# Layer norms shifted by four chunks' mean, with compact statistics, in a decoder layer on one core

## The chip, the cores and the metric

One core of one Trainium2 chip. Times are device microseconds (us) of one execution; the median of three runs of the kernel before is 938.13 us (937.85 to 939.4).

## What is computed

One decoder layer for 256 prompt rows and 64 sample rows (8 sequences of 8), width 1024, all fp32. Cut to the parts that matter:

```python
def _layernorm(x, g, b):
    mu = jnp.mean(xf, -1, keepdims=True)
    var = jnp.mean(jnp.square(xf - mu), -1, keepdims=True)
    y = (xf - mu) * lax.rsqrt(var + LN_EPS) * g + b

def mod(t, i):
    return t * (1.0 + ada[:, i, 1, None, :]) + ada[:, i, 0, None, :]

def post(t, y, i):
    return _layernorm(DEEPNORM_ALPHA * t + ada[:, i, 2, None, :] * y, ln_g[i], ln_b[i])

x = post(x, 0.5 * _swiglu(mod(x, 0), f1g, f1u, f1d), 0)
m, st = mixer(mod(x, 1))          # q, k, v, glu projection; attention over a paged cache; convolution
x = post(x, m, 1)
x = post(x, 0.5 * _swiglu(mod(x, 2), f2g, f2u, f2d), 2)
```

## The kernel before, in words

**Layout.** Activations are kept transposed: width over 128 partitions and 8 chunks, 320 rows along the free side (`xT`, `yT`, `uT`, one chunk 128x320). Every product runs in three fp32r matmuls (high x high, high x low, low x high), so each weight unit of 2048 columns of bytes (256 output columns, 1 MB) is loaded to `raw`, rounded to `whi` by ScalarE (`hi`, line 656) and its rest put into `wlo` by VectorE (`lo`, line 973). A unit's product is two halves (cc 0 and 1) of 24 matmuls of 320 columns (`product`, lines 1409 to 1411); `products` (lines 1422 to 1424) does several targets chunk by chunk, as the chunks' high (`mh`) and low (`ml`) parts come from a norm.

**Stages**, each in order on TensorE: adaptive parameters (`ada`), FFN 1 up (UP1, 22 units) and down (DN1, 12 units), input projection (WIN, 10 units, with the prompt's attention between), the cache stage (64 chunks of 1 MB of cached keys and values in a ring of 8 slots, loaded through SyncE's queue; four pairs of sequences, `pair_keys` and `pair_values`), output projection (WOUT, 4 units), FFN 2 (UP2, DN2), and the rows out. The order of each engine is written out by hand; semaphores tie them. SyncE's loads stand in one queue and each waits until its slot is free.

**Slots.** `whi` and `wlo` have two slots, `whi2` and `wlo2` are a third. They share memory with the cache stage's buffers: `whi` with `kT`, `wlo` with `kvw` (ring slots 6 and 7), `whi2` and `wlo2` with `araw` (ring slots 4 and 5, and in FFN 1 the landing place of the ada weights). `slot_w` names the slot of a unit, `slot_before` the unit that must be used up before its high half may be written. Output weights 0 and 1 are loaded before the last values, to `araw`, while values 4 and 5 of the last pair go to `kvw`; so the low half of output unit 0, which is written to `kvw`'s memory, waits until these values are used (`v_used`).

**A norm before.** `add_residual` (lines 1025 to 1027) makes `yT` chunk by chunk from the last products and from `xT`, which GpSimd has scaled by alpha (`scale_x`, line 582). GpSimd sums chunks 0 to 6 (`y_sums`, line 577); TensorE multiplies this sum and chunk 7 with a matrix of 1/1024, which gives the mean in every partition (lines 1498, 1500). VectorE subtracts it in four passes of two chunks (line 1081), ScalarE squares (738), VectorE adds the squares by pairs (1085), TensorE sums them over partitions (1504), ScalarE takes the root (740), VectorE the reciprocal over 128x320 (1088). Then per chunk: scaling (1093), modulation for the next stage from folded parameters (`fold_g`, `fold_b`; 1103 to 1105), high part by ScalarE (745), low part by VectorE (1019), and the new `xT` with gain and bias by ScalarE (747). Between, `keep_clock` gives TensorE matmuls of no use (1494). One low half of the next stage stands between the squares' sums and the reciprocal.

**The end of the cache stage.** `pair_values(3)` works on 8 values as they land. Before the last value `conv_half(0, 0, 4)` does 24 matmuls of output unit 0 on the convolution's chunks; the same of unit 1, in two parts around `attn_turn(3)`, follows the last value. Then the attention's chunks for both units together, then units 2 and 3.

## Time and profile before

| | us |
|---|---|
| median of 3 runs | 938.13 |
| the profiled execution | 937.36 |
| its span | 935.5 |
| TensorE busy | 854.9 |
| VectorE busy | 470.2 |
| ScalarE busy | 343.2 |
| GpSimd busy | 267.1 |

The span runs from the first to the last instruction; the execution's time is 1.9 us longer. Matmuls are pipelined and their shown ends overlap, so distances are read from start to start. An idle time with the engine and line that ended it stands in brackets behind a row. The times of all rows are those of this one execution.

### The profile page before, as it was taken

Reading aid. Unit: us, or ns where it says so; the run is one execution under the profiler, and the core shown is the slowest. Engines: PE = TensorE matmul, PEld = TensorE weight load, DVE = VectorE, ACT = ScalarE, POOL = GpSimd, SP = SyncE. Lnnn points to the kernel's source line nnn. Section 1 sums busy time; section 2 is a strip of 40 time slices with the busy share of each in tenths; the row PEclk is TensorE's granted clock in tenths of the full one; section 3 lists DMA queues with packets and bytes.
Section 4 is the critical chain, followed back from the end, with each engine's and each line's share of the span. In section 5 each row is a group of like instructions: output and inputs, shape, how many; then the busy total and the mean of one; then the engine's idle time right before and its main releaser. Section 6 shows DMA issues by size and latency. Waiting matters only on the chain.

```text
span 935.5 us, 16896 instructions
## 1 busy us (share of the span) xinstructions
PE 854.9 (91%) x6712; PEld 751.9 (80%) x6712; DVE 470.2 (50%) x751; ACT 343.2 (37%) x465; POOL 267.1 (29%) x319
## 2 busy tenths in 40 slices
PE   5699999998799988999986889869889999999997
PEld 3499989997699968988764556538789999999995
DVE  1543433432233379753686776743773454453436
ACT  2323332331222255454443324363363433432223
POOL 2020000000010013999999999600220000000000
PEclk9599999999799999999999999989999999999999
DMA  9957778777677442433998999996414544634301
GB/s 305 350 191 259 231 231 258 230 232 255 206 234 244 150 142 84 152 126 119 348 319 265 365 350 374 348 347 222 134 54 138 171 135 147 195 125 158 124 1 57
DMA packets 181521, 195.87 MB, mean 209 GB/s; under 512 B 11811, under 2 KB 163609, under 8 KB 181445
## 3 DMA queue, kind: packets, MB, share of 16 engines
q1 hardware_dynamic: 174541, 188.47, 61.9%
q10 hardware_dynamic: 6624, 6.33, 2.1%
q8 instruction: 46, 0.75, 0.3%
q14 instruction: 22, 0.18, 0.1%
q0 software_dynamic: 288, 0.14, 0.1%
HBM read 192.09 MB, written 3.17 MB: 209 GB/s over the span
## 4 chain that ended last, share of the span: by engine, by line
PE 78%; DVE 11%; DMA 5%; ACT 3%; issue 2%; SPq 1%; ACTq 0%; DVEq 0%
PE bank L1409 19%; PE bank L1410 18%; PE bank L1411 18%; PE bank L1625 5%; PE bank L1385 3%; PE bank L1650 3%; PE bank L1720 2%; DVE wlo L973 2%; PE bank L1374 1%; PE bank L1422 1%; DVE kT L1214 1%; PE bank L1423 1%; PE bank L1424 1%; DMA raw<-in_w_ada 1%; DMA xrow<-in_x_sample 1%
## 5 line engine op out<-in xcount | busy, mean ns | idle before, releaser
L973 DVE TENSOR_TENSOR wlo<-raw,whi 128x2048 fp32r<-128x2048 f32 (+1 forms) x80 | 190.8, 2386 | 257.6 <-ACT whi L656 256.3
L1409 PE MATMUL bank<-mh,whi 128*128 128x320 f32 x824 | 261.0, 317 | 4.5 <-DVE wlo L973 4.5
L1411 PE MATMUL bank<-mh,wlo 128*128 128x320 f32 x824 | 255.5, 310 | 0.0
L1410 PE MATMUL bank<-ml,whi 128*128 128x320 f32 x824 | 255.4, 310 | 0.0
L656 ACT CAST whi<-raw 128x2048 fp32r<-128x2048 f32 (+1 forms) x80 | 148.5, 1861 | 258.6 <-PE bank L1411 171.3
L1409 PEld LDWEIGHTS bank<-mh,whi 128*128 128x128 f32 x824 | 155.7, 189 | 15.3 <-issue 10.3
L1410 PEld LDWEIGHTS bank<-ml,whi 128*128 128x128 f32 x824 | 155.9, 189 | 0.0
L1411 PEld LDWEIGHTS bank<-mh,wlo 128*128 128x128 f32 x824 | 155.5, 189 | 0.0
L1409 PE MATMUL bank<-hh,whi 128*128 128x320 f32 x352 | 109.7, 312 | 0.0
L1410 PE MATMUL bank<-hl,whi 128*128 128x320 f32 x352 | 108.6, 309 | 0.0
L1411 PE MATMUL bank<-hh,wlo 128*128 128x320 f32 x352 | 108.6, 308 | 0.0
L622 POOL TENSOR_SCALAR tmp<-cbuf,dwT 128x256 f32<-128x256 f32 x90 | 95.4, 1060 | 0.0
L629 POOL TENSOR_TENSOR yT<-yT,tmp 128x320 f32<-128x320 f32 x90 | 81.2, 903 | 7.5
L1409 PEld LDWEIGHTS bank<-hh,whi 128*128 128x128 f32 x352 | 66.0, 188 | 2.5 <-issue 2.1
L1410 PEld LDWEIGHTS bank<-hl,whi 128*128 128x128 f32 x352 | 66.0, 188 | 0.0
L1411 PEld LDWEIGHTS bank<-hh,wlo 128*128 128x128 f32 x352 | 66.0, 188 | 0.0
L577 POOL TENSOR_TENSOR tmp<-yT 128x320 f32<-128x320 f32 x3 | 2.6, 874 | 219.0 <-DVE yT L1027 219.0
L596 POOL TENSOR_TENSOR fold_g<-adaT,par 128x72 f32<-128x72 f32 x2 | 0.6, 316 | 207.9 <-DVE adaT L993 207.9
L866 ACT COPY kT<-bank 128x1024 f32<-128x1024 f32 x32 | 35.6, 1114 | 55.8 <-PE bank L1625 55.8
L714 ACT ACTIVATE tmp<-bank 128x320 f32<-128x320 f32 x44 | 19.3, 438 | 94.4 <-PE bank L1411 87.4
L1214 DVE COPY kT<-bank 128x1024 f32<-128x1024 f32 x30 | 36.6, 1221 | 28.4 <-PE bank L1625 28.3
L1048 DVE TENSOR_TENSOR tmp<-bank,tmp 128x320 f32<-128x320 f32 x44 | 21.4, 487 | 57.4 <-PE bank L1411 37.0
(237 smaller groups left out, 1151.8 us busy)
## 6 DMA issues: line engine op xcount, KB each, us to landing
araw<-in_w_ada SPq DMA_DIRECT2D x28, 1024.0 KB, 5.1
raw<-in_ffn_wg SPq DMA_DIRECT2D x22, 1024.0 KB, 7.1
raw<-in_ffn_wu SPq DMA_DIRECT2D x22, 1024.0 KB, 7.1
raw<-in_ffn_wd SPq DMA_DIRECT2D x16, 1024.0 KB, 6.5
raw<-in_cache_k SPq DMA_DIRECT2D x64, 256.0 KB, 4.7
raw<-in_cache_v SPq DMA_DIRECT2D x60, 256.0 KB, 5.2
raw<-in_w_in SPq DMA_DIRECT2D x10, 1024.0 KB, 5.2
raw<-in_w_ada SPq DMA_DIRECT2D x8, 1024.0 KB, 12.5
```

The costliest lines, as they stand in the source:

```text
L622: pool.tensor_scalar(to[:, 0:SEQ], cbuf[:, c, k:k + SEQ], w, *more)
L629: pool.tensor_tensor(acc_c, acc_c, to, ALU.add).then_inc(conv_ready if last else pool_step, 1)
L656: act.copy(wh(slot_w(phase, u))[:, 0:size], landed(phase, u)[:, 0:size]).then_inc(w_hi, 1)
L866: act.copy(kT_view(k, 0), bank_keys(0)).then_inc(kt_low, 1)
L973: dve.tensor_tensor(wl(slot_w(phase, u))[:, 0:size], landed(phase, u)[:, 0:size], wh(slot_w(phase, u))[:, 0:size].bitcast(F32), ALU.subtra ...
L1214: dve.tensor_copy(kT_view(k, 1), bank_keys(1)).then_inc(kt_high, 1)
L1385: ins = pe.matmul(bank[g:g + QG, b + a_ % 2, 0:UC], cT[:, kk, :], src[:, UC * kk:UC * kk + UC], start=kk < 4, stop=kk >= 4)
L1409: pe.matmul(bank[:, b, 0:T], wh(slot)[:, c], h_, start=(start and n == 0), stop=False)
L1410: pe.matmul(bank[:, b, 0:T], wh(slot)[:, c], l_, start=False, stop=False)
L1411: ins = pe.matmul(bank[:, b, 0:T], wl(slot)[:, c], h_, start=False, stop=(stop and n == len(parts) - 1))
L1625: ins = pe.transpose(bank[:, 2 * half + x // 2, to:to + P], slot[:, at:at + P], ident)
L1650: ins = pe.matmul(out, qb[:, 2 * j + k // 4, h, :], keys[:, :, :, h, :], start=e == 0, stop=e == 1)
```

## The change

Six things, all in one diff:

- **Shift.** After the first half of down unit 7 (of output unit 2 for norm 1) TensorE multiplies the sum of chunks 0 to 3 with the 1/1024 matrix. VectorE subtracts twice that, the mean of these four chunks, from `yT` chunks 0 to 3 and from `xT` chunks 4 to 7, so that all chunks come out shifted by a value near the mean. The variance is then the mean of the squares less the square of the shifted mean d.
- **Sums inside the last units.** ScalarE squares chunks 0 to 5 and GpSimd adds them up while the last units are multiplied (in norm 1 fewer: squares 4 and 5 come after the stage's last high half).
- **Compact statistics.** Sums over partitions go by `spread`: two matmuls of 64 output rows and 160 columns, so that the 320 rows' statistics lie as 128x160, each twice in scale of 1/16. Square of d, variance, root and reciprocal work on 160 columns; two matmuls put the reciprocal back into two banks for the scaling. d itself is summed in full and subtracted from `yT` by passes of two chunks (`centre`) between the scalings. A root of a single column (`warm`) is put ahead of the last squares.
- **Alpha** is multiplied into the gain and bias columns of norms 0 and 1; GpSimd's scaling of `xT` is left for the first stage only.
- **Projection.** WIN uses the slots in the order 2, 0, 1; its unit 0 no longer waits for a down unit, the last unit shares slot 0 with unit 7 and is converted after it. The low half of WIN unit 1 stands between the residuals of chunks 6 and 7 (UP2 unit 1: between chunks 5 and 6). In the output projection the attention's chunks are done unit by unit; the first two units of UP2 are done as four targets together.
- **Swap.** Values 4 and 5 of the last pair go to `araw`, output weights 0 and 1 to `kvw`; the low halves of these are written over the landed weights, with no wait for values. `conv_half(0)` moves to behind value 5, the first half of `conv_half(1)` to behind value 6. In norm 2 VectorE makes every second output chunk.

```diff
 def kv_slot(kvi):
-    return kvi % KV_RING if kvi < KVN - 8 else (0, 1, 2, 3, 6, 7, 2, 3)[kvi - KVN + 8]
+    return kvi % KV_RING if kvi < KVN - 8 else (0, 1, 2, 3, 4, 5, 2, 3)[kvi - KVN + 8]
 def slot_w(phase, u):
     if phase[0] == WIN[0]:
-        return u % 3
+        return 0 if u == WIN[2] - 1 else (2, 0, 1)[u % 3]
 def slot_before(phase, u):
     if phase[0] == WIN[0]:
-        return phase[0] + u - (2 if u < 2 else 3)
+        if u == 0:
+            return -1
+        return phase[0] + u - (2 if u == WIN[2] - 1 else 3)
     if phase[0] == WOUT[0]:
-        return (WIN[0] + 9, WIN[0] + 7, WIN[0] + 8, WOUT[0])[u]
+        return (WIN[0] + 9, WIN[0] + 8, WIN[0] + 6, WOUT[0])[u]
+NORM_BANKS = ((6, 4, 5, 6, 5), (4, 5, 6, 7, 4), (6, 4, 5, 6, 5))
+HG, NSPREAD = 64, T // 2
...
         # SyncE
-                    sp.wait_ge(w_used, WIN[0] + (9, 9, 10, 8)[kvi - RING])
+                    sp.wait_ge(w_used, WIN[0] + (7, 7, 10, 9)[kvi - RING])
-                        sp.wait_ge(v_used, 16 + 5 + u)
-                        sp.dma_start(araw[:, u, :]...)
+                        sp.wait_ge(v_used, 16 + 7 + u)
+                        sp.dma_start(kvw[:, u, :]...)
...
         # GpSimd
+            def late_sum(n):
+                pool.wait_ge(y_ready, 8 * n + 6)
+                pool.wait_ge(shift_ready, n + 1)
+                pool.tensor_tensor(tmp[:, 3, :], yT[:, 4, :], yT[:, 5, :], ALU.add).then_inc(ysum_step, 1)
+            def square_sum(n, q):
+                pool.wait_ge(sq_ready, 8 * n + q + 1)
+                if q > 1:
+                    pool.wait_ge(sqsum_step, 5 * n + q - 1)
+                pool.tensor_tensor(tmp[:, 2, :], tmp[:, 0, :] if q == 1 else tmp[:, 2, :], tmp[:, q % 2, :], ALU.add).then_inc(sqsum_step, 1)
+            def norm(n):
+                y_sums(n)                      # now chunks 0 to 3
+                for q in range(1, 5):
+                    square_sum(n, q)
+                late_sum(n)
+                square_sum(n, 5)
+            pool.tensor_scalar(par1[:, 72:88], par1[:, 72:88], ALPHA, None, ALU.mult)
+            pool.tensor_scalar(par1[:, 96:112], par1[:, 96:112], ALPHA, None, ALU.mult).then_inc(fold_ready, 1)
-            scale_x(1)
-            scale_x(2)
...
         # ScalarE, in down() of the FFNs
+                    if u == 7:
+                        for q in range(4):
+                            square(n, q)
+                    if u == 9:
+                        square(n, 4)
+                        square(n, 5)
+            def norm(n, first, meanwhile=lambda: None):
+                act.activation(warm[:, :], con[:, C_EPS:C_EPS + 1], ACT.Sqrt)
+                for q in range(first, NCH):
+                    square(n, q)
+                act.wait_ge(rest_ready, n + 1)
+                act.activation(tmp[:, 0, 0:NSPREAD], bank[:, NORM_BANKS[n][2], 0:NSPREAD], ACT.Square).then_inc(dsq_ready, 1)
+                act.wait_ge(vd_ready, n + 1)
+                act.activation(tmp[:, 0, 0:NSPREAD], tmp[:, 0, 0:NSPREAD], ACT.Sqrt, scale=16.0 ** -2, ...).then_inc(std_ready, 1)
+                meanwhile()                    # norm 0: high half of WIN unit 2
...
         # VectorE
+            def shift(n):
+                sums = bank[:, NORM_BANKS[n][0]:NORM_BANKS[n][0] + 1, 0:T].to_broadcast([P, 2, T])
+                dve.wait_ge(shift_ready, n + 1)
+                for q in (0, 1):
+                    y = yT[:, 2 * q:2 * q + 2, :]
+                    dve.scalar_tensor_tensor(y, sums, -2.0, y, ALU.mult, ALU.add).then_inc(yc_ready, 1)
+                for q in (2, 3):
+                    x = xT[:, 2 * q:2 * q + 2, :]
+                    dve.scalar_tensor_tensor(x, sums, -2.0, x, ALU.mult, ALU.add).then_inc(xs_ready, 1)
                 # down(), before the low half of unit u + 2
+                    if u == 7:
+                        shift(sub)
                 # output projection
-                if u < 2:
-                    lo(WOUT, u + 2)
-                elif u == 3:
+            lo(WOUT, 2)                        # ahead of the loop
+                if u == 2:
                     lo(UP2, 0)
+                    shift(1)
+                    if n == 1:
+                        lo(WOUT, 3)
+                    if n == 5:
+                        lo(UP2, 1)
                 # norm()
+                dve.tensor_tensor(small[0], bank[:, NORM_BANKS[n][3], 0:NSPREAD], small[0], ALU.subtract).then_inc(vd_ready, 1)
+                dve.reciprocal(small[1], small[0]).then_inc(nr_ready, 1)
+                dve.wait_ge(mean_ready, n + 1)
+                centre(0)                      # centre(1..3) ahead of the scaling of chunks 2, 4, 6
+                dve.wait_ge(spread_mm, 2 * n + 2)
...
         # TensorE, first FFN 2 products
-                        products([(0, ...), (1, ...), (2, ...)], ...)
-                        product(3, slot_w(phase, 1), 1, m_parts(range(NCH))).then_inc(w_used, 1)
+                        products([(2 * x + cc, ...) for x in range(2) for cc in range(2)], ...)
+            def shift(n):
+                pe.wait_ge(ysum_step, 4 * n + 3)
+                pe.matmul(bank[:, NORM_BANKS[n][0], 0:T], lnones, tmp[:, 3, :], start=True, stop=True).then_inc(shift_ready, 1)
             # norm(n), after the last product
+                pe.wait_ge(y_ready, 8 * n + 7)
+                pe.wait_ge(ysum_step, 4 * n + 4)
+                spread(rest, tmp[:, 3, :], 0)
+                pe.wait_ge(sqsum_step, 5 * n + 5)
+                spread(sq, tmp[:, 2, :], 0)
+                spread(rest, yT[:, 6, :], 1)
+                pe.wait_ge(sq_ready, 8 * n + 7)
+                spread(sq, tmp[:, 0, :], 1)
+                pe.wait_ge(y_ready, 8 * n + 8)
+                spread(rest, yT[:, 7, :], 2).then_inc(rest_ready, 1)
+                pe.wait_ge(sq_ready, 8 * n + 8)
+                spread(sq, tmp[:, 1, :], 2).then_inc(var_ready, 1)
+                ...                            # full mean: three matmuls; the reciprocal back: two
+                keep_clock(2, 5)
-            pair_values(3, {2: group_scales, 6: lambda: conv_half(0, 0, NCC)})
-            conv_half(1, 0, 2)
+            pair_values(3, {2: group_scales, 5: lambda: conv_half(0, 0, NCC), 6: lambda: conv_half(1, 0, 2)})
+            conv_half(1, 2, 3)
             attn_turn(3)
-            conv_half(1, 2, NCC)
-            products(first, ...)
+            conv_half(1, 3, NCC)
+            for u in range(2):
+                products(first[2 * u:2 * u + 2], ...)
             ...
+                    if u == 2 and cc == 0:
+                        shift(1)
```

## Rows read from the trace of the kernel before

**Rows 1.** Page, part 1: busy time, share and instructions of each engine.

```profile
PE 854.9 (91%) x6712; PEld 751.9 (80%) x6712; DVE 470.2 (50%) x751; ACT 343.2 (37%) x465; POOL 267.1 (29%) x319
```

**Rows 2.** Busy by stretch (instructions); last: TensorE's granted clock, DMA share, GB/s.

```profile
602.00:622.00 20.00, 16.96 (x230) 9.71 (x230) 8.00 (x15) 13.07 (x22) 0.00 (x0) 1.00 1.09 346
622.00:632.00 10.00, 3.78 (x40) 1.41 (x44) 6.34 (x6) 5.61 (x8) 0.00 (x0) 0.68 1.10 348
680.00:697.00 17.00, 15.52 (x95) 15.24 (x95) 11.67 (x30) 12.03 (x18) 6.69 (x1) 0.90 0.01 2
```

**Rows 3.** TensorE in order of time: start, length, line, [idle before and releaser]; norm 0, projection.

```profile
336.22 0.78 PE L1498 MATMUL bank<-tmp,con 128*128 128x320 f32 x2 [0.56 <-POOL tmp L577]
...
350.07 0.39 PE L1422 MATMUL bank<-mh,whi 128*128 128x320 f32 x1 [2.30 <-DVE ml L1019]
...
364.09 0.31 PE L1424 MATMUL bank<-mh,wlo 128*128 128x320 f32 x1
367.39 0.41 PE L1409 MATMUL bank<-mh,whi 128*128 128x320 f32 x1 [2.99 <-DVE wlo L973]
...
431.36 0.41 PE L1409 MATMUL bank<-mh,whi 128*128 128x320 f32 x1
...
442.71 0.98 PE L1625 MATMUL bank<-con,raw 128*128 128x128 f32 x7
```

**Rows 4.** VectorE in order of time, from norm 0's mean on.

```profile
337.57 3.01 DVE L1081 TENSOR_TENSOR yT<-yT,bank 128x640 f32<-128x640 f32 x4 [1.00 <-PE bank L1500]
...
342.41 2.28 DVE L973 TENSOR_TENSOR wlo<-raw,whi 128x2048 fp32r<-128x2048 f32 x1
344.61 2.15 DVE L1088 RECIPROCAL tmp<-tmp 128x320 f32<-128x320 f32 x1
...
349.44 0.48 DVE L1019 TENSOR_TENSOR ml<-uT,mh 128x320 fp32r<-128x320 f32 x1
...
358.17 1.10 DVE L1019 TENSOR_TENSOR ml<-uT,mh 128x320 fp32r<-128x320 f32 x2
...
359.41 10.12 DVE L973 TENSOR_TENSOR wlo<-raw,whi 128x2048 fp32r<-128x2048 f32 x2
```

**Rows 5.** ScalarE in order of time, norm 0.

```profile
339.36 1.35 ACT L738 ACTIVATE tmp<-yT 128x640 f32<-128x640 f32 x2
...
341.99 1.28 ACT L740 ACT_TABLE_LOAD   x1
```

**Rows 6.** GpSimd in order of time, behind norm 0.

```profile
359.39 6.68 POOL L582 TENSOR_SCALAR xT<-xT 128x2560 f32<-128x2560 f32 x1 [20.54 <-ACT xT L747]
```

**Rows 7.** TensorE, then VectorE, in order of time, end of the cache stage.

```profile
603.15 2.42 PE L1773 MATMUL bank<-yT,con 128*128 128x320 f32 x8
...
623.98 1.07 PE L1720 MATMUL bank<-kvw,pT 128*32 128x256 f32 x16 [3.24 <-DMA kvw<-in_cache_v]
...
631.23 1.94 PE L1720 MATMUL bank<-raw,pT 128*32 128x256 f32 x16 [2.30 <-DMA raw<-in_cache_v]
...
625.19 2.29 DVE L973 TENSOR_TENSOR wlo<-araw,whi 128x2048 fp32r<-128x2048 f32 x1 [4.11 <-PE bank L1720]
```

**Rows 8.** TensorE in order of time, around norms 1 and 2.

```profile
664.99 0.70 PE L1498 MATMUL bank<-tmp,con 128*128 128x320 f32 x2
...
679.16 0.38 PE L1422 MATMUL bank<-mh,whi 128*128 128x320 f32 x1 [2.00 <-DVE ml L1019]
...
696.49 0.41 PE L1409 MATMUL bank<-mh,whi 128*128 128x320 f32 x1 [1.48 <-DVE wlo L973]
...
914.83 0.70 PE L1498 MATMUL bank<-tmp,con 128*128 128x320 f32 x2
```

**Rows 9.** VectorE and GpSimd in order of time, last unit of the output projection.

```profile
658.94 2.29 DVE L973 TENSOR_TENSOR wlo<-raw,whi 128x2048 fp32r<-128x2048 f32 x1
...
659.10 2.86 POOL L577 TENSOR_TENSOR tmp<-tmp,yT 128x320 f32<-128x320 f32 x1 [0.67 <-DVE yT L1027]
662.62 0.88 POOL L577 TENSOR_TENSOR tmp<-tmp,yT 128x320 f32<-128x320 f32 x1 [0.66 <-DVE yT L1027]
```

**Rows 10.** VectorE in order of time, norm 2: the scaling of all eight chunks.

```profile
925.48 3.31 DVE L1093 TENSOR_TENSOR yT<-yT,tmp 128x320 f32<-128x320 f32 x8
```

169 lines of the change are left out of this document (101 added, 68 removed).

## The prediction

> **What bounds the kernel now.** I read the page first: TensorE is busy for 91% of the span, the next engine for half [rows 1]. So the end is set by TensorE's own work and by the places where it waits, and only those can be shortened. The table of stretches then shows that the cache stage is another thing: from 602 to 622 the DMA queues are full (share 1.09) while TensorE is not, and at the end of that stage (1.10) the granted clock drops to 0.68 [rows 2]. Then TensorE's order of time at the three layer norms: each is a hole. In norm 0 its products end at 335.66 (the wait of 0.56 before 336.22), and the next real product is at 350.07, 14.4 us later; norm 1 runs from 664.99 to 679.16, 14.2 us; norm 2 from 914.83 to the end [rows 3, 8]. What fills the hole is VectorE [rows 4]: four subtractions of the mean (3.01), sums of squares, a low half (2.28), a reciprocal over 320 columns (2.15), then scaling and modulation; the low part of chunk 0 starts at 349.44. Behind norm 0 is a second stall of 2.99: the low halves of the input projection's units 2 and 3 took 10.12 us together where one takes 2.28, beside GpSimd's scaling of x from 359.39 to 366.07 [rows 3, 4, 6]. At the end of the cache stage TensorE waits 3.24 us for values 4 of the last pair and 2.30 for values 6, and the first low half of the output projection waits 4.11 us for TensorE [rows 7].
>
> **Scaling of x gone (alpha is folded into gain and bias).** It removes 6.68 us of GpSimd in two places, which cover nothing else. Without it the low half of unit 2 takes 2.2 us from its start.
>
> **Norm 0.** Price list: a matmul of 320 columns against the ones matrix is two records, 0.70 us with the tail of the last, which the next covers: 0.6 [rows 8]. A "spread" sum is two matmuls of 160 columns to different output halves: 0.3 us if they overlap, 0.58 if not; I take 0.35, since the value products, to four outputs of 32 rows, do overlap: 16 records of 256 columns in 1.07, 0.067 each [rows 7], where a full one of 320 takes 0.1476. A reciprocal of 160 columns is between half of 2.15 and that plus a fixed part: 1.15. A centring pass of two chunks is 3.01/4 = 0.75, the shift pass (the same shape with one PSUM source) the same, 1.0 at worst [rows 4].
> The shift matmul adds 0.6 to the products, so they end at 336.25 (P). The shift passes (3 us of VectorE), squares of chunks 0 to 5 and GpSimd's sums lie under products of units 7 to 11, where VectorE is idle for 5 us and more between low halves; free, or up to 1 us if one holds back a low half. The projection's unit 0 now goes to the third weight slot, free early; the low half of unit 1 moves between the residuals of chunks 6 and 7, so y7 is ready at P+1.35 and no longer at P+0.9, for 2.2 us less later. From there, one after the other: last spread 0.4, its square 0.4, subtraction 0.35, root 0.4 (two squares of 640 take 1.35 [rows 5]), reciprocal 1.15, first centring 0.75, then on VectorE two scalings, the modulation of chunk 0, one centring, a scaling, the modulation of chunk 1 and the low part of chunk 0, 3.9 (from the period of 1.52 per chunk: seven low parts lie between 349.44 and the pair at 358.17, plus 0.85 for the centring [rows 4]). TensorE restarts at P+9.0 = 345.25, after 9.0 where it was 14.4: **5.4 less**, 0.6 of it given back to the shift matmul.
> The first projection is 96 matmuls at (364.09 - 350.07)/95 = 0.1476, 14.17 us [rows 3]. VectorE now spends 1.52 + 0.43 per chunk against 1.77 of TensorE, so two short waits come back: +0.6. It ends at 360.0. The low half of unit 2 is then 357.1 to 359.4 and no one waits: the hole of 3.15 between 364.24 and 367.39 is gone. Sum: 5.4 - 0.6 - 0.6 + 3.15 = **7.35**.
>
> **Does that arrive?** The projection behind it is TensorE's work throughout. The last unit runs from 431.36 to 442.71; unit 8, of equal length, begins at about 420, and only then the last unit's high half may start: its low half is there at about 424.7, 6.7 before it is needed [rows 3]. SyncE's queue now holds cached keys 3 until then (old: 415), but keys 4 and 5 may follow at once instead of waiting for 430; key products start at 442.7. All loads of the cache stage wait for slots freed by this chain, so the full DMA stream moves with it. GpSimd's convolution has ended before 602 (no GpSimd work from there on [rows 2]), TensorE needs it at 603.15 [rows 7], and it starts 7 us earlier too.
>
> **Last values and output weights swap.** Loads keep their order and the queue is what they wait for, so values 4 to 7 land when they did. The low halves of the projection's units 0 and 1 no longer wait for values (4.11 gone); they are written over their own landed weights at about 621 and 628. So 24 matmuls can stand between values 5 and 6, where TensorE idles 2.30 [rows 7]. Half of them run at half clock as before. The products behind the conv part start 2.95 earlier, with 0.5 lost since only 6 matmuls cover the last turn.
>
> **Output projection and norm 1.** Unit by unit, unit 0 ends half a product stage earlier; VectorE takes the low half of unit 2 (now behind the low parts) until 645.9, residuals 0 and 1, the low half of unit 3 until 649.75, residuals 2 and 3 until 651.35, then a low half of the next stage. The shift matmul stands behind the first half of unit 2 (651.55) and needs GpSimd's third sum. In the trace a GpSimd sum of 0.88 that began 0.16 after a low half took 2.86, ending 0.76 after it [rows 9]. Here the same happens: the third sum ends at 654.6, TensorE waits **3.05**, then 0.6 for the matmul. Without the block the wait is 0.95. So the stage ends at 2.95 - 3.65 = 0.7 later than now. Then the hole is 8.7 instead of 14.2: 5.5 less. In the first FFN products, four targets together instead of three and one: 14.17 us, 1.7 of half clock as now (0.90 over 17 us [rows 2]), 0.2; but the last 24 matmuls no longer cover activation, high half and low half of unit 2: those end about 3.9 after the last product, where the wait was 1.48 [rows 8]. 20.0 instead of 17.3: 2.7 lost. Net: -0.7 + 5.5 - 2.7 = **2.1**.
>
> **Norm 2.** Shift matmul: 0.6 lost. Reciprocal done at P+3.85, first centring P+4.6; then 3 centrings, 8 scalings and 4 of the 8 affines on VectorE, 7.4: P+12.0. Now the scalings end at 928.8 = P+13.9 [rows 10], and the copies to rows follow on the same engine in both. **2.1 less**, -0.6.
>
> **A rule weighed.** In the trace one change of ScalarE's function table costs 1.28, at 341.99, under VectorE's work [rows 5]; a dummy root now pulls it ahead. But squares now stand between that root and the real one. The Trainium skill (ScalarE: Activation LUTs, Table sets: the hidden batching unit) says that functions come in sets, that a switch costs about 2.7 us, and names relu, copy, identity and abs as present in every set; square isn't in that list. By it, were square missing beside the root, each norm would pay two more switches. The trace speaks against it: the squares from 339.36 ran before the root's load, with the table that Silu had left.
> A second: by the rows the low half beside GpSimd's scaling ran from 359.41 and both ended at 369.53, so about 5.7 us were lost, not the 6.66 that were left of it. The Trainium skill (SBUF — State Buffer, SBUF: two separate sides) has the port locked for the whole instruction; by that rule the pair would have ended at 370.5, and the gain be the same, as TensorE only waits for the first.
>
> **Rivals.** (A) *GpSimd's sums are not blocked* at the output projection: 2.1 more, 925.1. For: the sum may be issued first. Against: rows 9. 0.12.
> (B) *The clock falls* once more than now, behind norm 0 or in the 3 us wait at the output projection: 1.7 each [rows 2], 929 to 930.6. For: norm 1 shows it. Against: the holes are shorter. 0.12.
> (C) *Square and root are in different tables*: two more loads of 1.28 in each norm, one of them in the chain after the variance, the other partly: about 1.6 per norm, 932. 0.06.
> (D) *The cache stage does not move*, because its stream is full from start to end and something that didn't move starts it: 7.35 lost, 934.6. Against: its loads wait for low halves and units of the projection. 0.08.
> (E) *Slower*: the last unit of the input projection. ScalarE does its high half in the midst of exponentials and table loads, VectorE the low half after; TensorE and, through SyncE's one queue, all cached keys behind key 3 wait for it. Up to 6.7 us late costs nothing, each later one its own length; slower than before by over 0.2% needs 6.7 + 11 + 2 = 20 us late: 941. 0.03.
> (F) The stages are shorter in the profile and the end isn't, 937 to 939: 0.04.
>
> **Numbers.** 7.35 + 2.1 - 0.6 + 2.1 = 10.95. The profiled execution took 937.36 (span 935.5), so 926.4; the median of the runs stands 0.8 above it, so the forecast is 927.2 (chance 0.55, own range 925 to 929.5, from the spread sums, 0.25 each, and the wait at the shift). From A to C: 922.5 to 932.5, leaving out D, E, F and tails. 0.2% is about what a measurement can tell from no change: faster 0.92, same 0.04, slower 0.04.
>
> **What would show it.** Holes of 9.0 and 8.7 us between last and next product at norms 0 and 1; no wait before the first matmul of projection unit 2, whose start moves from 367.4 to 360; the first key product 7 us earlier; a wait of 1 to 3 us before the second shift matmul, named GpSimd, and a GpSimd sum of over 2 us there; 3.5 to 4 us before unit 2 of the second FFN; last scaling 12 us after the last product. Wrong it is if VectorE's period of 1.95 per chunk is over 2.1, if the spreads cost 0.6 each (1 us per norm), or if table loads stand in the norms' chain.

## The result, and the profile after

The changed kernel takes **932.88 us** (median of 6 runs, 931.35 to 934.13), the one before 938.93 on the same chip (6 runs, 937.85 to 941.01): ratio 0.9933, 95% interval 0.9916 to 0.9950. It is faster by 6.05 us where 10.95 were forecast. It lies 3.4 us above the range given for the sum (925 to 929.5) and 0.4 us above the wide one (922.5 to 932.5). A second set of runs (after_again) gave 933.84 against 939.28, ratio 0.9939 (0.9916 to 0.9961).

One thing of the kernel must be said more plainly than it was: the compact statistics hold columns 0 to 159 of the rows' sums in 64 partitions and columns 160 to 319 in the other 64, so that square, root and reciprocal run over 160 columns in place of 320.

The page of the changed kernel, busy time by engine and the granted clock in 40 slices, to be laid beside [rows 1]:

```profile
span 932.3 us, 17017 instructions
PE 854.9 (92%) x6742; PEld 752.2 (81%) x6742; DVE 470.7 (50%) x758; ACT 343.6 (37%) x479; POOL 271.6 (29%) x328
PEclk9599999999699999999999899989999999999999
```

TensorE is still the bound. Norm 0 in TensorE's order of time (start, length, engine, line, operation, what ended the idle time before it) answers to [rows 3]:

```profile
341.44 0.77 PE L1598 MATMUL bank<-tmp,con 128*64 128x160 f32 x8
342.03 0.44 PE L1598 MATMUL bank<-yT,con 128*64 128x160 f32 x4
...
345.89 0.54 PE L1620 MATMUL bank<-tmp,con 64*128 64x160 f32 x4 [0.26 <-DVE tmp L1158]
346.36 2.96 PE L1590 MATMUL bank<-con 128*128 128x320 f32 x10
350.77 0.39 PE L1509 MATMUL bank<-mh,whi 128*128 128x320 f32 x1 [1.45 <-DVE ml L1071]
...
365.61 0.30 PE L1496 MATMUL bank<-mh,whi 128*128 128x320 f32 x1
```

The hole, the time from the norm's first sum to the next stage's first product, is 350.77 - 341.44 = 9.3 us (forecast 9.0; before, 14.4), and unit 2 starts at 365.61 with no wait, 24.2 us behind the last product; before it was 31.7 with a wait of 2.99. VectorE in the same hole, to be laid beside [rows 4]:

```profile
343.87 0.32 DVE L1156 TENSOR_TENSOR tmp<-bank,tmp 128x160 f32<-128x160 f32 x1 [1.10 <-PE bank L1598]
344.69 1.15 DVE L1158 RECIPROCAL tmp<-tmp 128x160 f32<-128x160 f32 x1 [0.49 <-ACT tmp L790]
345.75 0.76 DVE L1152 TENSOR_TENSOR yT<-yT,bank 128x640 f32<-128x640 f32 x1
...
350.14 0.48 DVE L1071 TENSOR_TENSOR ml<-uT,mh 128x320 fp32r<-128x320 f32 x1
```

The reciprocal is 1.15 and the centring 0.76, as bounded; from the end of the centring (346.5) to the first product 4.3 us pass where 3.9 were forecast.

The output projection is the stage furthest from the forecast. TensorE, GpSimd and VectorE around the second shift matmul:

```profile
652.42 1.27 PE L1553 MATMUL bank<-tmp,con 128*128 128x320 f32 x2 [2.77 <-POOL tmp L586]
653.02 0.94 PE L1496 MATMUL bank<-mh,whi 128*128 128x320 f32 x1
653.76 0.47 PE L1497 MATMUL bank<-ml,whi 128*128 128x320 f32 x1
...
648.40 0.87 POOL L586 TENSOR_TENSOR tmp<-tmp,yT 128x320 f32<-128x320 f32 x1 [0.16 <-DVE yT L1079]
649.44 2.84 POOL L586 TENSOR_TENSOR tmp<-tmp,yT 128x320 f32<-128x320 f32 x1 [0.16 <-DVE yT L1079]
...
649.28 2.28 DVE L1025 TENSOR_TENSOR wlo<-raw,whi 128x2048 fp32r<-128x2048 f32 x1
653.73 1.56 DVE L1117 SCALAR_TENSOR_TENSOR yT<-bank,yT 128x640 f32<-128x640 f32 x2 [2.17 <-PE bank L1553]
```

The wait is 2.77 (forecast 3.05), and its cause is the forecast one: the sum that takes 0.87 alone took 2.84 beside the low half that began 0.16 ahead of it. But the matmuls behind it take 0.47 where 0.31 is usual: the clock has fallen. The table of stretches (busy us of each engine, then granted clock, DMA share, GB/s) shows it, and again behind the wait before unit 2 of the second FFN:

```profile
648.00:652.00 4.00, 1.65 (x12) 1.38 (x10) 3.49 (x6) 0.13 (x1) 3.67 (x3) 1.00 0.89 273
652.00:656.00 4.00, 3.58 (x12) 3.22 (x13) 2.27 (x4) 0.83 (x2) 0.79 (x2) 0.57 0.83 255
656.00:660.00 4.00, 4.00 (x29) 4.00 (x28) 2.73 (x8) 2.44 (x3) 2.12 (x3) 1.00 0.07 19
689.00:693.00 4.00, 0.25 (x2) 0.00 (x0) 2.33 (x2) 3.43 (x2) 0.00 (x0) 1.00 0.01 2
693.00:697.00 4.00, 3.99 (x17) 3.99 (x17) 3.76 (x5) 0.86 (x2) 0.00 (x0) 0.57 0.64 203
```

A granted clock of 0.57 over 3.6 to 4.0 busy us is 1.5 to 1.7 us lost at each of the two places: in those stretches TensorE ran partly at 1.2 and partly at 2.4 GHz. Who waits for whom before that unit, in ScalarE, VectorE and TensorE:

```profile
687.97 0.88 ACT L744 ACTIVATE tmp<-bank 128x320 f32<-128x320 f32 x2 [1.49 <-PE bank L1511]
688.74 3.69 ACT L686 CAST whi<-raw 128x2048 fp32r<-128x2048 f32 x2
...
690.66 2.29 DVE L1025 TENSOR_TENSOR wlo<-raw,whi 128x2048 fp32r<-128x2048 f32 x1 [5.52 <-ACT whi L686]
...
693.01 0.42 PE L1496 MATMUL bank<-mh,whi 128*128 128x320 f32 x1 [3.76 <-DVE wlo L1025]
```

ScalarE first waits for unit 0's last product (the Silus), only then makes the high half, and VectorE waits 5.52 for that.

**By segments.** One pair of profiles is too little here: the runs of one kernel lie 3 us apart. So each unedited kernel was profiled several times (experiments below). Each segment runs from one row of TensorE to another; us, mean of five profiles before and four after, ranges in brackets. The indented lines split the one above them at the first product of the output projection that uses the attention's chunks:

```
segment                                     before                   after                    change  forecast
start to first product, first down proj.    250.4 (249.1 to 252.2)   250.9 (249.0 to 252.7)   +0.5     0
to its last product                          86.06 (all)              87.6 (86.8 to 88.5)     +1.5    +0.6
hole of norm 0                               14.72 (all)               9.57 (all)             -5.15   -5.4
to the group means (projection, cache)      254.3 (253.1 to 256.5)   250.3 (249.8 to 251.5)   -4.0    -2.55
to the last product, output projection       61.1 (58.6 to 62.6)      64.7 (64.0 to 65.3)     +3.6    +0.7
  up to the attention's chunks (conv part)   40.1 (37.6 to 41.7)      38.5 (37.8 to 39.1)     -1.6    -2.95
  from there on                              20.98 (all)              26.20 (all)             +5.2    +3.65
hole of norm 1                               14.33 (all)               9.22 (all)             -5.1    -5.5
second FFN                                  235.53 (all)             239.2 (239.0 to 239.7)   +3.7    +3.3
tail (norm 2, stores)                        20.85 (20.8 to 20.9)     19.08 (19.0 to 19.1)    -1.8    -2.1
sum                                         937.3                    930.6                    -6.65  -10.95
```

The holes are counted from the start of the last product, so they are 0.2 to 0.3 longer than in the text. This table is the measure for all that follows: it puts two thirds of the miss into the output projection. Behind the conv part every profile of a kernel gives the same length to 0.02 us, so there one profile is enough. Before the split the same kernel varies by 4 us, and the change of 1.6 can't be told from chance. The first row behind the split, in the profile after:

```profile
638.82 0.42 PE L1509 MATMUL bank<-mh,whi 128*128 128x320 f32 x1 [0.42 <-DVE ml L1397]
```

### The profile page after: what moved, and what is told of

It is laid out like the page before. It is cut to its first block, busy times and chain, and to the rows that moved or that the text cites. A ratio compares the mean times of both kernels' runs of the same rounds, so it can differ in the third digit from the quotient of the medians.

```text
span 932.3 us, 17017 instructions
## 1 busy us (share of the span) xinstructions
PE 854.9 (92%) x6742; PEld 752.2 (81%) x6742; DVE 470.7 (50%) x758; ACT 343.6 (37%) x479; POOL 271.6 (29%) x328
## 4 chain that ended last, share of the span: by engine, by line
PE 74%; DVE 12%; DMA 6%; ACT 2%; issue 2%; SPq 2%; POOL 0%; ACTq 0%; DVEq 0%
PE bank L1496 18%; PE bank L1498 18%; PE bank L1497 18%; PE bank L1741 5%; PE bank L1472 3%; PE bank L1766 3%; DMA raw<-in_ffn_wu 2%; DMA raw<-in_w_ada 2%; DVE kT L1297 1%; PE bank L1509 1%; PE bank L1836 1%; DVE wlo L1025 1%; PE bank L1461 1%; DMA raw<-in_ffn_wg 1%; DVE yT L1170 1%
## 5 line engine op out<-in xcount | busy, mean ns | idle before, releaser
L1025 DVE TENSOR_TENSOR wlo<-raw,whi 128x2048 fp32r<-128x2048 f32 (+1 forms) x80 | 184.0, 2300 | 259.6 <-ACT whi L686 259.5
L653 POOL TENSOR_SCALAR tmp<-cbuf,dwT 128x256 f32<-128x256 f32 x90 | 90.9, 1010 | 0.0
L660 POOL TENSOR_TENSOR yT<-yT,tmp 128x320 f32<-128x320 f32 x90 | 84.0, 934 | 7.5
L586 POOL TENSOR_TENSOR tmp<-yT 128x320 f32<-128x320 f32 x3 | 4.6, 1517 | 242.7 <-DVE yT L1079 242.7
```

The source lines that it names most:

```text
L653: pool.tensor_scalar(to[:, 0:SEQ], cbuf[:, c, k:k + SEQ], w, *more)
L660: pool.tensor_tensor(acc_c, acc_c, to, ALU.add).then_inc(conv_ready if last else pool_step, 1)
L1025: dve.tensor_tensor(wl(slot_w(phase, u))[:, 0:size], landed(phase, u)[:, 0:size], wh(slot_w(phase, u))[:, 0:size].bitcast(F32), ALU.subtra ...
```

## The experiments

**Is it the change, or the day?** The profile after reached the first down projection 3.4 us later than the one before (252.66 against 249.30), in code that is the same. So both kernels ran again, unedited.

> The changed kernel once more, nothing edited. Its profiled execution reached the first product of the first down projection 5.15 us later than the one of the kernel before (261.95 against 256.80), in code that the change does not touch, with the granted clock at half in 250.8 to 256.5. Theory P (the clock's falls move from execution to execution): this time that point lies between 256.5 and 262, not at the same value to 0.2 us, and the median is again near 932.9 (931.5 to 934). Rival Q (the change itself causes it, through addresses or the order of loads): the point is again at 261.8 to 262.1 and the falls stand at the same places. Of the two falls behind the shift matmul of the output projection (653.8) and behind unit 2 of the second FFN (693.8): if they follow from the waits of 2.8 and 3.8 us ahead of them they stand there again, 1.3 to 1.6 us each.

> The kernel before once more, nothing edited. Theory P: the start of the down projection (256.80 in the profile shown) lies somewhere between 256.5 and 262, later than 257.5 with even chances, and the time is 937.5 to 941. Rival Q: it lies at 256.7 to 256.9, and only the changed kernel ever loses the 5 us.

Measured: after_again 933.84 us, segment start 251.77; before_again span 938.0, 249.09. The fall at 250 to 256 was gone, but the two falls behind the waits stood where they had been (652 and 693). In before_again the wait of 3.00 before unit 2 of the projection was followed by a fall that the profile I predicted from lacks. The table of stretches of before_again, then of the kernel before:

```profile
366.00:376.00 10.00, 8.81 (x45) 8.80 (x45) 6.46 (x7) 2.82 (x4) 0.84 (x2) 0.66 0.83 263
```

```profile
366.00:376.00 10.00, 8.61 (x61) 8.61 (x62) 6.66 (x7) 3.45 (x6) 3.22 (x7) 1.00 0.79 258
```

The next suspect for the late start was the table of constants, one column wider in the changed kernel. Two kernels: the one before with a dead column more (before_wider), the changed one with the constant in a small tile instead (after_narrow).

```
-C_N = C_GOUT + P
+C_N = C_GOUT + P + 1
```

```
-C_EPSQ = C_GOUT + P
-C_N = C_EPSQ + 1
+C_N = C_GOUT + P
...
             scale_x()
+            pool.memset(warm[:, 1:2], EPS / 256)
...
-                act.activation(tmp[:, 0, 0:NSPREAD], tmp[:, 0, 0:NSPREAD], ACT.Sqrt, scale=16.0 ** -2, bias=con[:, C_EPSQ:C_EPSQ + 1])
+                act.activation(tmp[:, 0, 0:NSPREAD], tmp[:, 0, 0:NSPREAD], ACT.Sqrt, scale=16.0 ** -2, bias=warm[:, 1:2])
```

> The kernel before, with one unused column more in the table of constants (1979 instead of 1978 columns of 4 bytes, as in the changed kernel), nothing else. In both profiles of the kernel before the clock falls at 14 to 18 us, is back at 45.8 and falls at 233; in all four of the changed kernel and its variants it doesn't fall at 14, comes back at 46.5 to 48.9 and falls at 234 to 236, and the first down projection starts 1.3 to 3.4 us later, in code that is the same. Theory W (the width moves the first loads by some tenths, and with them the phase of the clock's falls): this kernel shows the pattern of the changed one and takes 1.5 to 3 us more than the one before: median 940.5 to 942. Rival X (it is something else in the changed program, or chance): same pattern and same time as before, 938.5 to 939.8.

> The changed kernel, with the constant EPS/256 written by GpSimd into a small tile and no longer a column of the table of constants, which has its old width again. Theory W: the pattern at the start is that of the kernel before (fall at 14 to 18, clock back at 45.8), the first down projection starts at 249 to 250, the median is 1.5 to 3 us below the changed kernel's: 930 to 931.5. Rival X: nothing changes, 932.5 to 933.8.

Measured: before_wider 941.14 (ratio 1.0024, 1.0009 to 1.0039), segment start 251.29; after_narrow 933.08 (0.9934, 0.9911 to 0.9958), segment start 249.73. The two contradict each other: adding the column seems to cost 1.9 us, taking it away gives nothing. The width is not shown to be the cause. Then three more profiles of the kernel before and two of the changed one:

> The kernel before a third time, unedited. In both earlier profiles the first down projection starts at 249.1 to 249.3, in the eight of edited kernels at 249.7 to 252.7, mean 251.2, in code that none of them changed there; the table's width didn't explain it (alpha_alone has the old width and 250.9). Theory P (chance): as likely above 249.7 as below. Rival Q (every edited program is 2 us late at that point, by where its instructions or data lie): 249.0 to 249.4 again, with the fall of the clock at 14 to 18 and its return at 45.8. Between norm 0 and the group means: 254.8 to 255.0 if the clock falls behind the wait of 3 us before projection unit 2 (as in two of three profiles with that wait), 253.1 if not.

> The kernel before, unedited. Theory P (chance): start of the first down projection anywhere from 249 to 252.5. Rival Q (it belongs to the changed program): 249.0 to 250.2 again. From norm 0's first product to the group means 254.8 to 256.5 with a fall of the clock at 366 to 376 (two of three profiles), or 253.1 without.

> As before_fourth. Theory P: the start of the first down projection lies above 250.5 in one of the two. Rival Q: in neither.

> The changed kernel, unedited. Theory P: start of the first down projection anywhere from 249 to 252.5, no fall of the clock at 249 to 257. Rival Q: 251.5 to 252.7. A fall of the clock behind the shift matmul of the output projection with 3 chances in 4, then 64.3 to 65.3 us from the group means to the last product, else 60.3 to 63.

> As after_third. Theory P: the start of the first down projection lies below 251 in one of the two. Rival Q: in neither. Behind unit 2 of the second FFN the clock falls again (every profile with the wait of 3.76 shows it, neither of the two without).

Measured: segment start 250.18, 252.19 and 251.12 before, 250.21 and 248.96 after. The ranges overlap, so up to that point the difference is chance: 249.30 against 252.66 was a low draw beside a high one. In after_third and after_fourth both falls behind the waits were there again. What stays open is a fall at 248 to 257, at the start of the first down projection: 5 of 11 profiles of the changed kernel and its variants have it, none of 7 of the kernel before and its variants. It makes the down projection 1.5 to 1.8 longer each time (88.3 to 88.5 instead of 86.8). The products that it falls on were not edited, and its cause wasn't found.

The profiled execution of after_narrow needs a word, since it is used below. It took 927.31 us, the lowest of its six (median 933.08). It is the only profile with the full wait at the second shift matmul and no fall behind it, and its conv part took 35.7 us, at full clock from 620 to 634; the four unedited profiles have a fall at the end of the cache stage (between 617 and 629).

**Alpha alone.** The kernel before with the two scalings of x gone (the waits that went with them are left out here):

```
+            pool.tensor_scalar(par1[:, 72:88], par1[:, 72:88], ALPHA, None, ALU.mult)
+            pool.tensor_scalar(par1[:, 96:112], par1[:, 96:112], ALPHA, None, ALU.mult).then_inc(fold_ready, 1)
...
-            scale_x(1)
...
-            scale_x(2)
...
```

> The kernel before, with alpha folded into gain and bias (GpSimd's two scalings of x gone), nothing else. Theory: the low half of unit 2 behind norm 0 takes 2.3 us instead of its share of 10.12, unit 2 of the projection starts at 364.4 instead of 367.39 and the rest follows: 3.0 less; behind norm 1 the wait of 1.48 before unit 2 stays, ScalarE's high half being late there. Median 936.3. Rival (the cache stage is bound by its own stream): the 3 us are lost by the first value product and the median is 938.5 to 939.5. Rival (the scaling was no part of the stall; VectorE was late by itself): no gain at unit 2, 939.

Measured: 933.97 us (ratio 0.9945, 0.9924 to 0.9965), 5.25 less than before: more than the 3.0 expected, and nearly what the whole change brings. Its segment from norm 0 to the group means is 248.6, against 253.1 to 256.5. Of these 5.7 the stall accounts for 3.15. Another 1.15 is the clock: from unit 2 to the first key product the kernel before takes 75.3 us in three profiles and 77.9 to 78.0 in the two with a fall at 366 to 374 (before_wider: 78.1, with one); alpha_alone takes 75.2, without. So such a fall costs 2.6. The last 1.4 lie in the cache stage (159.2 against 159.6 to 161.3) and are not resolved by one profile. The second FFN is 0.75 shorter (the wait before unit 2 is 0.72 instead of 1.48).

The whole change, with five things more, has the ratio 0.9933 (0.9916 to 0.9950): the intervals overlap, so what the other five things bring together isn't told from nothing. Laid beside alpha_alone's one profile, the table shows why. The two holes and the tail are 12.0 us shorter, and the rest is 11.8 longer: 1.5 in the first down projection, 1.8 in projection and cache stage, 4.1 in the output projection, 4.4 in the second FFN.

**The shift matmul of norm 1.** Three edits of the same place. First, behind the second half of unit 2:

```
-                    if u == 2 and cc == 0:
+                    if u == 2 and cc == 1:
                         shift(1)
```

> The changed kernel, with the shift matmul of norm 1 behind the second half of unit 2 of the output projection instead of behind the first. Theory S (the wait of 2.77 us for GpSimd's third sum costs its length, and the clock's fall right behind it costs 1.3 to 1.6 more): no wait there, the stage ends 2.5 to 2.8 earlier by the wait and 1.4 by the clock, together 4 us less than the changed kernel: median 928.9. Rival T (VectorE's chain ends the stage anyway: shift passes, residuals 4 and 5, low half, residuals 6 and 7): the products end earlier and the hole of norm 1 grows by as much, median 932 to 933. Rival U (the wait goes, the fall of the clock stays, here or elsewhere): 930.1.

Measured: 932.61 (0.9927, 0.9903 to 0.9951), forecast 928.9: no gain that can be told. No wait, no fall, and the part behind the conv products is 21.6 instead of 26.2, but the hole of norm 1 grew from 9.2 to 12.1: rival T, VectorE's chain ends the stage. The wait before unit 2 of the FFN was followed by a longer fall (239.8 for the FFN). Next, the same wait filled with work whose result isn't used:

```
                     if u == 2 and cc == 0:
+                        keep_clock(5, 4)
                         shift(1)
```

> The changed kernel, with four matmuls against the ones matrix (2.4 us of TensorE, their result not used) between the first half of unit 2 of the output projection and the shift matmul, in the time in which TensorE waits for GpSimd's third sum. It does the same work otherwise. Theory B (the fall of the clock at 652 to 656 follows from the idle 2.8 us; three of four profiles show it): no fall there, the stage from the group means to the last product takes 62.8 to 63.8 instead of 64.3 to 65.3, the median is 1.3 us lower, 931.8. Rival (the falls come at their own times, whatever TensorE did just before): a fall in that place or elsewhere as often as before, median 932.5 to 933.8. The wait for the sum itself stays: filler and wait together 2.8.

Measured: 932.71 (0.9919, 0.9899 to 0.9940), forecast 931.8. Its row of the stretch that shows 0.57 above:

```profile
652.00:656.00 4.00, 4.00 (x27) 3.84 (x27) 3.37 (x5) 1.50 (x4) 0.99 (x2) 1.00 0.85 266
```

The shift matmul stands at its usual time and no fall follows; the part behind the conv products is 24.62 instead of 26.20, 1.58 less, as theory B has it. This is one profile, and the fall stayed away once with the full wait too (after_narrow, 24.64). So the claim that the idle time brings the fall rests on the count over all kernels, further down. The median isn't lower by more than the measurement can tell. In the profiled execution the second FFN had the longer fall (239.8) and the first down projection had one (88.5); whether the other executions lost the gain in that way isn't shown. Third, the cause of the wait taken away: VectorE takes the low half of the next stage behind the shift passes. This one has the edit of high_early too (below).

```
                 if u == 2:
-                    lo(UP2, 0)
                     shift(1)
+                    lo(UP2, 0)
```

> high_early (927.2) with one more move: in the output projection VectorE takes the low half of unit 0 of the second FFN behind its four shift passes and not ahead of them. Theory G (this low half, started 0.16 ahead of GpSimd's third sum, is what stretches that sum from 0.87 to 2.84): the sum takes 0.87 and ends 2.0 earlier, TensorE's wait at the shift matmul is 0.7 to 0.9 instead of 2.78, the shift passes start 2.0 earlier, and the output projection ends 1.9 earlier, 3.4 where the clock would have fallen behind the wait: median 924.5. Rival H (the stretch comes from elsewhere): the sum still takes 2.8, nothing gained, 927. Rival I (the square sums, 0.87 and 1.90 in GpSimd at 655.5, now fall beside that low half and are stretched by 2, and the first product behind norm 1 waits for them): wait gone, hole of norm 1 longer by 1 to 2 us, 926.

Measured: **924.38 us** (0.9841, 0.9822 to 0.9861), forecast 924.5. The rows of sum_free, GpSimd and TensorE:

```profile
646.31 0.86 POOL L586 TENSOR_TENSOR tmp<-tmp,yT 128x320 f32<-128x320 f32 x1 [0.16 <-DVE yT L1080]
...
651.41 3.81 POOL L599 TENSOR_TENSOR tmp<-tmp 128x320 f32<-128x320 f32 x2 [0.64 <-ACT tmp L765]
...
647.31 0.78 PE L1554 MATMUL bank<-tmp,con 128*128 128x320 f32 x2 [0.79 <-POOL tmp L586]
```

The third sum takes 0.86 instead of 2.84, the wait 0.79 instead of 2.77, and no fall follows: theory G. The part behind the conv products is 22.65 instead of high_early's 26.22, 3.6 less (forecast 3.4). The low half now stretches one of two square sums (3.81 for both) instead, and the next low half another; the hole of norm 1 is 1.1 longer (10.3 instead of 9.2), so rival I was half right as well.

**The high half of unit 2 of the second FFN**, made by ScalarE inside norm 1:

```
-            norm(1, 4)
+            norm(1, 4, lambda: hi(UP2, 2))
...
-                    hi_next(2)
+                    if ffn == 0 or pair_:
+                        hi_next(2)
```

> The changed kernel, with ScalarE's high half of unit 2 of the second FFN taken inside norm 1, behind the root (where ScalarE idles 3.6 us before the first chunk), and no longer behind the Silus of unit 0. Theory: the wait of 3.76 us before unit 2 was ScalarE's order: it ran the two Silus (687.97, they wait for unit 0's last product at 687) ahead of the high half, and VectorE's low half then waited 5.5 for that. With the high half at 668.2 the low half follows the last low part at 685.1 and lands at 687.4, before unit 1 ends at about 689.2: no wait, 3.5 to 3.8 less, and the fall of the clock behind it (693.8, 1.5 us) goes as well: 5.0 less, median 927.9. Rival: VectorE is late anyway or the fall stays: 3.7 less, 929.2. Rival: the next pair of units waits instead (units 3 and 4), less than 1 us gained: 932.

Measured: 927.17 (0.9879, 0.9854 to 0.9903), forecast 927.9. Its rows, ScalarE, VectorE, TensorE:

```profile
666.47 1.88 ACT L686 CAST whi<-raw 128x2048 fp32r<-128x2048 f32 x1
...
683.49 2.29 DVE L1026 TENSOR_TENSOR wlo<-raw,whi 128x2048 fp32r<-128x2048 f32 x1
...
687.52 0.31 PE L1497 MATMUL bank<-mh,whi 128*128 128x320 f32 x1
```

The low half follows the last low part, unit 2 starts without a wait and at full clock, and the FFN takes 233.5 instead of 239.0 to 239.7: 3.76 of wait, 1.5 of clock, 0.3 more. Then all three moves together, with VectorE's low half of FFN unit 1 behind the last residual:

```
                     if n == 1:
                         lo(WOUT, 3)
-                    if n == 5:
-                        lo(UP2, 1)
+            lo(UP2, 1)
             norm(1)
```

> The changed kernel with three moves: the high half of unit 2 of the second FFN inside norm 1 (as in high_early), the shift matmul of norm 1 behind the second half of unit 2 (as in shift_later), and VectorE's low half of unit 1 of the second FFN behind the residual of chunk 7 instead of between chunks 5 and 6. In shift_later the products ended 4 us earlier, but the first product behind norm 1 came only 0.2 earlier (73.3 us behind the group means instead of 73.55): VectorE's low half at 660.3 to 662.6 stood ahead of residuals 6 and 7. Theory: with it behind, residual 7 ends 2.3 earlier and the low half fits in the wait for the last spread sums except for 0.6 to 0.9 us: 1.4 to 1.7 less, and the fall of the clock behind the shift stays away (1.5): together with high_early (927.2) median 924.3. Rival 1: only the clock's part or only the order's part comes: 925.8. Rival 2: GpSimd's late sums, now beside the low half, are blocked and take the gain: 927.

Measured: 929.22 (0.9893, 0.9866 to 0.9919), slower than high_early alone (forecast 924.3): rival 2, and worse than the 927 it said. VectorE, GpSimd and TensorE:

```profile
660.79 2.96 DVE L1026 TENSOR_TENSOR wlo<-raw,whi 128x2048 fp32r<-128x2048 f32 x1
...
661.57 2.90 POOL L599 TENSOR_TENSOR tmp<-tmp 128x320 f32<-128x320 f32 x1
...
664.52 0.80 PE L1598 MATMUL bank<-tmp,con 128*64 128x160 f32 x4 [1.97 <-POOL tmp L599]
```

TensorE waits 2.14 for a GpSimd sum and, one spread later, 1.97 for the last square sum, which the low half stretches (0.87 alone). The clock falls at the end of the first of these waits (0.63 in 661 to 664, 0.50 in 664 to 668), so the spreads run at half clock (0.80 where 0.44 to 0.49 is usual), and the hole is 15.7 instead of 9.2.

**The place of the conv products.** TensorE's order at the end of the cache stage as before, slots and loads as in the changed kernel:

```
-            pair_values(3, {2: group_scales, 5: lambda: conv_half(0, 0, NCC), 6: lambda: conv_half(1, 0, 2)})
-            conv_half(1, 2, 3)
+            pair_values(3, {2: group_scales, 6: lambda: conv_half(0, 0, NCC)})
+            conv_half(1, 0, 2)
             attn_turn(3)
-            conv_half(1, 3, NCC)
-            for u in range(2):
-                products(first[2 * u:2 * u + 2], m_parts(MIX_ORDER[NCC:]), lambda n: pe.wait_ge(ml_ready, 16 + NCC + n + 1), start=False)
+            conv_half(1, 2, NCC)
+            products(first, m_parts(MIX_ORDER[NCC:]), lambda n: pe.wait_ge(ml_ready, 16 + NCC + n + 1), start=False)
```

> The changed kernel, with TensorE's order at the end of the cache stage as before: the conv half of unit 0 between values 6 and 7, the attention half for both units together. The prediction gave the placing 2.95 us, because the products fill the 2.3 us that TensorE waits for values 6. Theory: the stage from the group means to the last product of the output projection is 2.5 to 3 longer than the changed kernel's 64.3 to 65.3; median 935.5 to 936. Rival (the wait before the shift matmul, which is VectorE's and GpSimd's, takes it up, since that chain starts with unit 0's end): all of the attention half comes for four targets at once, unit 0 is ready a half stage later and the wait at the shift stays 2.8: 937 or more. Rival (the values' transfers vary by as much): less than 1 us, 933.5.

Measured: 935.96 (0.9961, 0.9947 to 0.9976), 2.1 to 3.1 above the changed kernel. The output projection is 69.84 instead of 64.7, 5.1 longer in this profile. Up to the attention's chunks it is 41.1 instead of 38.5, which is within what one kernel varies there. From there on it is 28.74 instead of 26.20, and that is clear; 2.1 of these 2.5 are the wait at the shift matmul:

```profile
653.65 1.41 PE L1553 MATMUL bank<-tmp,con 128*128 128x320 f32 x2 [4.90 <-POOL tmp L586]
```

The rest is a longer fall of the clock, from 651 within that wait to 658. In the conv part TensorE still waits 1.07 for values 6 here. The median bears out the size of the forecast for the placing (2.95), but not its reason: what is clear of chance is that unit 0 ends earlier and with it the chain of residuals and sums; what the filled wait itself brings isn't resolved.

## Why the prediction was wrong

**The norms were right.** The holes are 5.15 and 5.1 shorter (forecast 5.4 and 5.5). The terms listed for norm 0 add up to 8.7 and not to the 9.0 written; measured are 9.3, since the way from the last residual (342.78) to the subtraction takes 1.1 instead of 0.8 and the one from the centring to the first product 4.3 instead of 3.9. VectorE's period is 1.95 per chunk, as forecast. The tail is 1.8 shorter; the prediction wrote 2.1, but its own P+13.9 and P+12.0 give 1.9. The shift matmul costs 0.70 (0.6): in every profile without a chance fall the first down projection is 86.77 instead of 86.06. The 96 products with VectorE ahead of them take 14.84 (14.17 + 0.6 forecast). Spreads take 0.27 to 0.4, no table load was added (11 in both profiles; rival C is out), the stall of 2.99 is gone and the cache stage moved with it (rival D is out; group means at 600.70 for a projection that began at 350.77).

**The step that failed** is the sum's term for the output projection: it put 3.65 for the new wait and the matmul and nothing for the clock behind that wait, which stood among the rivals (B) at 0.12. The part behind the conv products took 20.98 in every profile before. In after_narrow, where the clock didn't fall, it took 24.64: 3.65 more. That this is the forecast to the hundredth is luck, the wait being 2.78 and not 3.05 and the rest 0.27 more. In all four profiles of the changed kernel the clock did fall, and the part took 26.20: 1.57 more, where the prediction priced such a fall at 1.7. I knew the price and the place and gave it 0.12. The argument against it, that the holes are shorter, was about other places; this wait was new, and the forecast itself had put 3 us there. It isn't the whole miss: rival B with one fall gives 929, and 932.88 was measured. Counted over all kernels: behind a wait of 2.77 or more at the shift the clock fell in 6 of 7 profiles, without it in 0 of 4; behind the wait of 3.76 before FFN unit 2 in 8 of 8, without it in 0 of 3.

At the second place the forecast had a fall in its sum, ahead of unit 2 where a wait absorbs it (in the kernel before the FFN takes 235.53 with a fall at 680, the wait before unit 2 being 1.5, and without, the wait being 2.1); it came behind the wait, where nothing does. There the first products were quicker instead (18.76 to unit 2, forecast 20.0), and by luck the two errors cancel: 3.7 for 3.3.

The rest of the output projection's miss of 2.9 is 1.3 in the conv part. It is 1.6 shorter on the mean and not 2.95: 2.58 by the two profiles laid side by side, but the kernel before was on the mean 0.6 quicker than in the profile used and the changed one 0.4 slower than in its first. No run resolves this term.

**The base was a single execution.** Against the forecast of 927.2 the time is 5.7 higher: 4.3 by the table above (2.9 of it the output projection, 0.9 the first down projection with its unexplained falls, 0.5 the start, 1.0 the two holes and the tail together, 0.4 the second FFN, less 1.4 that the projection and the cache stage gained more than forecast), 0.8 because the median before is 938.93 and not 938.13, 0.6 because medians and means of few runs differ. Of the gain of 1.4, 1.05 is rival B seen from the other side: the old wait of 2.99 also brought the clock down, 2.6 us each time, in two of the five profiles, but not in the one that was read.

**Point by point.** Holes 9.0 and 8.7: 9.3 and 9.0. Unit 2 without wait at 360: without wait, 24.2 behind the last product (23.75 forecast). First key product 7 us earlier: 1.9 earlier on that profile's clock, but the whole gain behind norm 0 is carried (99.4 us behind the last product instead of 107.05). Wait of 1 to 3 named GpSimd and a sum over 2 us: 2.77 and 2.84. 3.5 to 4 before FFN unit 2: 3.76, along the chain that was named (activation, high half, low half); that the high half need not stand behind the activation is what high_early shows. Last scaling 12 us behind the last product: 11.8.

## What to carry to other kernels

A new wait of TensorE can cost its length and then once more what the clock loses with it: here 1.57 us for 2.8 us of waiting in 5 of 6 profiles, and about as much or more for 3.76 us in 8 of 8. At such odds it belongs in the sum and not among the rivals. So the first look after such a change goes to the engines that feed the wait: two moves of order, one on ScalarE and one on VectorE, with no work added or removed, took the changed kernel from 932.9 to 924.4. And a sum of effects of 1 us each is to be set against several profiles of the kernel before, segment by segment: two executions of one kernel differ by 3 us without any change.

## What the runs showed of the hardware

VectorE's low halves and GpSimd's sums block one another in the order in which they start. The sum at 649.44 began 0.16 behind the low half and took 2.84; with 0.87 of own work after the low half's end at 651.56 it would end at 652.43, and it ended at 652.28. The Trainium skill (SBUF — State Buffer, SBUF: two separate sides) has the shared pair of ports as an exclusive lock that the first takes for its whole instruction; the trace agrees within 0.15 us. A pair in the kernel before agrees less well: the low half that began 0.02 behind GpSimd's scaling of 6.68 us ended 1.26 us after it, where 2.28 alone is usual, so it had got on by 1 us.

```profile
359.41 7.92 DVE L973 TENSOR_TENSOR wlo<-raw,whi 128x2048 fp32r<-128x2048 f32 x1
```

The blocking works the other way round too: in all_moved the low half began while GpSimd summed and took 2.96 instead of 2.29. The shift passes, whose one source lies in PSUM, did not do this: a GpSimd square sum at 655.49 took 0.87 beside one of them (655.20, 1.54).

The fall of the clock mostly begins just behind the wait, so the products pay for it (0.57 in 652 to 656 for a wait from 649.7 to 652.4). In some profiles it begins within the wait and then reaches further into the products: in after_third TensorE waits until 689.98, and the clock is at half before that; the second FFN takes 239.7 there instead of 239.0.

```profile
688.00:690.00 2.00, 0.02 (x1) 0.02 (x1) 2.00 (x2) 1.40 (x1) 0.00 (x0) 0.53 0.02 4
690.00:694.00 4.00, 4.00 (x15) 4.00 (x16) 3.72 (x5) 0.85 (x2) 0.00 (x0) 0.50 0.70 207
```

Whether it comes at all can differ between executions of one program: behind the 3.0 us wait of the kernel before it came in two of five profiles. In all_moved it came behind a wait of 2.14; behind 0.62 (shift_filled) and 0.79 (sum_free) none came.
